# Gather and scatter of an expert name all 128 rows with a bound on the row number; no size variants, counts or branches in GpSimd's loop

## The chip, the cores and the metric

One Trainium2 chip, one of its cores. The metric is the device time of one launch, in microseconds. Three runs of the kernel before took 1130.07, 1128.4 and 1129.77 us; the median is 1129.77 us.

## The reference, cut to what matters

One layer of a streaming encoder over 512 tokens of width 1024. A mixing sub-layer (mLSTM heads and sparse attention heads behind one projection) comes first; the change does not touch it. The channel sub-layer is a mixture of 64 small experts, eight of which each token selects:

```
scores = sigmoid(hf @ w_router);  sel = scores + b_router
the 4 best of 8 groups of experts, then the 8 best experts in them -> eidx (512, 8)
gw = scores[eidx] / sum * 2.5
for each expert e, for its tokens tok:
    xb = hf[tok]
    u  = silu(xb @ w_gate[e]) * (xb @ w_up[e])        # 1024 -> 256
    y[tok] += (u @ w_down[e]) * gate                  # 256 -> 1024
out = x + gate2 * rms_norm(y + shared expert)
```

512 x 8 selections over 64 experts are 64 tokens for an expert on average. For the reference's inputs the smallest expert has 37 tokens and the largest 100. All is float32; the weights of one expert are 3 x 1024 x 256 x 4 B = 3.15 MB, which are read from HBM once.

## The kernel before, in words

Three stages run before the experts: `stage_in`, `stage_attention`, `stage_route`. The last computes the routing, stores the normalised tokens as rows in HBM (`G.h2_rows`, 512 rows of 4 KB), and leaves tables in SBUF: for each token and expert its place in that expert, and with `G.count_tab` (L1417, L2165) the number of tokens of each expert.

`stage_experts` (from L1534) runs the 64 experts in order; each engine has its own loop, eight experts to a turn (`UNROLL`, `turns` at L1678), and they meet through semaphores. An expert has a tile of 128 rows (`CAP`): its tokens stand in partitions 0 to n-1, the rest is padding. For an expert e:

- VectorE builds one-hot picks (L1881), TensorE finds the token and gate of each place with them (L2017), and `pick_rows` (L1578) writes the row numbers `sidx`: token number for a place that is taken, and 512 + partition for a place that is not.
- GpSimd gathers the rows from `h2_rows` into `xg` with an indirect DMA (`gather_rows`, L1586), four experts ahead. A row number over 511 is out of bounds, and the row is left as it is.
- TensorE transposes the rows (L2024), ScalarE and VectorE split them and the weights in a high and a low float32r part (L1802, L1810, L1901, L1905), TensorE multiplies by gate and up (L2034, 24 matmuls), transposes u (L2042) and multiplies by down (L2089, 8 matmuls). This always works on 128 rows, whatever the count.
- ScalarE and VectorE scale the two halves of the result into `yb` (L1851, L1954; two buffers, each waits for the scatter two experts before), and GpSimd scatters the rows with an accumulating indirect DMA into `G.y_sums` in HBM (`add_rows`, L1592). The scatter before has to have landed first (L1770), since two of them may add to one row.
- SyncE issues the weight loads: gate and up of expert e+4 in halves as the split of expert e is done (L1692 to L1697), down of e+3 after the down product of expert e-1 (L1702). Four slots hold weights.

The last two experts' results are not scattered but added on TensorE (L2134). Then y is read back and normalised.

In GpSimd's loop (L1759) each gather and each scatter is written eleven times, for 48, 56, 64, ... 120 and 128 rows (`SIZES`, L51). `count_of` loads the expert's count into a register (L1757), and `by_size` (L1745) picks the variant with a tree of three or four branches (L1751, L1753). A variant's row lists, source and destination are cut to that many partitions. A scatter has no bound on its row number: the padding within its size is added to rows 512 to 639 of `y_sums`, which nobody reads. The first four gathers (L1742), ahead of the loop, name all 128 rows.

Of the kernel before, what the change touches and what calls it, by code (L numbers as in the profile page):

```python
# [22 lines left out]
SEQ = 512  # L23
# [11 lines left out]
E_N = 64  # L35
# [10 lines left out]
CAP = P  # L46
MAX_EXTRA = SEQ * 8 // CAP
STEPS = (SEQ - 1) // CAP
MEAN = SEQ * 8 // E_N

SIZES = [*range(MEAN - 16, CAP, 8), CAP]  # L51

QK_W = 2 * HEADS * DH
# [1056 lines left out]
def stage_route(nc, A, G):  # L1111

    with ExitStack() as own:  # L1113
# [179 lines left out]
        def _(dve):  # L1293
# [120 lines left out]

            n_e, k_e, cum, at = (cnt[:, n, :] for n in range(4))
            step(nc.vector.tensor_copy(n_e, ps[:, 7, NT * E_N:(NT + 1) * E_N]))
            nc.vector.tensor_copy(G.count_tab[:, :], n_e[0:1, :])  # L1417
            step(nc.vector.tensor_scalar(k_e, n_e, float(CAP), None, ALU.is_gt))
            for m in range(2, STEPS + 1):
                step(nc.vector.scalar_tensor_tensor(k_e, n_e, float(m * CAP), k_e, ALU.is_gt, ALU.add))  # L1420
# [113 lines left out]
def stage_experts(nc, A, G):  # L1534

    with ExitStack() as own:
# [46 lines left out]
            q(nc.vector.tensor_scalar(pad[:, 0:1], f, 0.0, k[0:CAP, K_PADROW:K_PADROW + 1], ALU.is_equal, ALU.mult))  # L1583
            return nc.vector.scalar_tensor_tensor(sidx[:, n:n + 1], f, -1.0, pad[:, 0:1], ALU.add, ALU.add)

        def gather_rows(pool, slot, n, rows=CAP):  # L1586

            return pool.indirect_dma_start(out=xg[slot][0:rows, :], out_offset=None, in_=G.h2_rows,  # L1588
                                           in_offset=bass.IndirectOffsetOnAxis(ap=sidx[0:rows, n:n + 1], axis=0),
                                           bounds_check=SEQ - 1, oob_is_err=False)  # L1590

        def add_rows(pool, slot, n, rows=CAP):  # L1592

            return pool.indirect_dma_start(out=G.y_sums, out_offset=bass.IndirectOffsetOnAxis(ap=sidx[0:rows, n:n + 1], axis=0),  # L1594
                                           in_=yb[0:rows, slot, :], in_offset=None, compute_op=ALU.add)

# [1 line left out]
        with ExitStack() as inner:  # L1600
# [129 lines left out]
            @block.gpsimd  # L1730
            def _(pool):
                for n in range(RING - 1):
                    nc.gpsimd.memset(xg[n], 0.0).then_inc(s_zero, 1)
                for n in range(2):
                    pool.dma_start(G.y_sums[SEQ + n * 64:SEQ + (n + 1) * 64, :], G.xt[0:64, 0, :]).then_inc(s_sc, 16)
                for n in range(AHEAD):
                    if n == RING - 1:
                        pool.wait_ge(s_sdn, NT)
                        nc.gpsimd.memset(xg[n], 0.0).then_inc(s_zero, 1)
                    pool.wait_ge(s_zero, n + 1)  # L1740
                    pool.wait_ge(s_idx, n + 1)
                    gather_rows(pool, n, n).then_inc(s_g[n], 16)  # L1742
                pool.wait_ge(s_yw, 16 * NT)

                def by_size(count, sizes, move):  # L1745

                    if len(sizes) == 1:
                        move(sizes[0])
                        return
                    half = len(sizes) // 2  # L1750
                    with pool.If(count > sizes[half - 1]):  # L1751
                        by_size(count, sizes[half:], move)
                    with pool.Else():  # L1753
                        by_size(count, sizes[:half], move)

                def count_of(e):
                    return pool.value_load(G.count_tab[0:1, bass.ds(e, 1)], min_val=0, max_val=SEQ)  # L1757

                def step(t, n, ahead):  # L1759
                    e = UNROLL * t + n  # L1760
                    if ahead(AHEAD):
                        pool.wait_ge(s_idx, e + AHEAD + 1)
                        pool.wait_ge(s_xp, e + 1)
                        pool.sem_inc(s_passed, 1)
                        count = count_of(e + AHEAD)
                        by_size(count, SIZES, lambda rows: gather_rows(pool, n % RING, (n + AHEAD) % UNROLL, rows).then_inc(s_g[n % RING], 16))
                    if ahead(2):
                        pool.wait_ge(s_ya, e + 2)
                        pool.wait_ge(s_yd, e + 2)
                        pool.wait_ge(s_sc, SC0 + 16 * e)  # L1770
                        pool.sem_inc(s_passed, 1)
                        count = count_of(e)
                        by_size(count, SIZES, lambda rows: add_rows(pool, n % 2, n, rows).then_inc(s_sc, 16))

                turns(pool, step)
                pool.sem_inc(x_added, 1)

                def extra(j):
                    pool.wait_ge(x_idx, j + 1)
                    pool.sem_inc(s_passed, 1)  # L1780
                    gather_rows(pool, 1, 0).then_inc(x_g, 16)
                    pool.wait_ge(x_ya, j + 1)
                    pool.wait_ge(x_yd, j + 1)
                    pool.sem_inc(s_passed, 1)
                    pool.indirect_dma_start(out=G.y_sums, out_offset=bass.IndirectOffsetOnAxis(ap=sidx[:, 0:1], axis=0),
                                            in_=xyb, in_offset=None, compute_op=ALU.add).then_inc(x_sc, 16)
                    pool.wait_ge(x_sc, 16 * j + 16)
                    pool.sem_inc(x_added, 1)

                extra_tiles(pool, extra, adds=True)  # L1790
# [352 lines left out]
def build(nc, A, out):  # L2143
    with ExitStack() as ctx:
        def sb(name, shape, dt=F32):
            return ctx.enter_context(nc.sbuf_tensor(name, shape, dt))

        G = Shared()
        G.ps = ctx.enter_context(nc.psum_tensor("ps", [P, 8, 512], F32))
        G.k = sb("consts", [P, K_W])  # L2150
        G.gb = sb("gate_bias", [HEADS, 2])
        G.cs = sb("cs", [P, KC])
        G.cols = sb("cols", [P, 44])
        G.rows = sb("rows", [P, 4, D])
        G.maskb = sb("maskb", [P, NT, SEQ])
        G.xt = sb("xt", [P, NT, D])
        G.s_wgu = [ctx.enter_context(nc.semaphore(f"gate_up_landed{n}")) for n in range(RING)]
        G.s_wd = [ctx.enter_context(nc.semaphore(f"down_landed{n}")) for n in range(RING)]
        G.s_wout = ctx.enter_context(nc.semaphore("w_out_landed"))

        G.u_shared = G.rows[:, 0, :].rearrange("p (f t) -> p f t", f=FC)
        G.posm = sb("place_in_expert", [P, E_N * NT])
        G.gt = sb("token_and_gate", [P, E_N, NT, 6], BF16)
        G.extra_base = sb("extra_base", [P, P])
        G.count_tab = sb("expert_counts", [1, E_N], I32)  # L2165
        G.extra_tab = sb("extra_tab", [1, P + 1], I32)
        G.h2_rows = nc.dram_tensor("h2_rows", (SEQ, D), F32, kind="Internal").ap()
        G.y_sums = nc.dram_tensor("y_rows", (SEQ + P, D), F32, kind="Internal").ap()
        G.out = out

        G.QKC = NT * NAT_W
        G.main = sb("main", [P, G.QKC + 2 * HEADS * SEQ])
        G.side = sb("side", [P, 10240])
        G.nat = G.main[:, 0:G.QKC].rearrange("p (i n) -> p i n", i=NT)
        G.qkc = G.main[:, G.QKC:].rearrange("p (c t) -> p c t", c=2 * HEADS)
        G.w_shared_down = G.main[:, G.QKC + 2048:G.QKC + 4096].rearrange("p (f n) -> p f n", f=FC)
        G.wout = G.side[:, 0:8192].rearrange("p (f n) -> p f n", f=2 * HEADS)
        G.row_pieces = [G.side[:, 8192:10240].rearrange("p (c d) -> p c d", c=2), G.xt[:, 1:3, :]]
        G.top8, G.last_left = G.xt[:, 3, 64:72], G.xt[:, 3, 128:128 + SEQ]  # L2180
        G.gf, G.ga = G.rows[0:HEADS, 3, 0:SEQ], G.rows[0:HEADS, 3, SEQ:2 * SEQ]
        G.aN = G.posm[:, 0:2 * NT * HEADS].rearrange("p (a i h) -> p a i h", a=2, i=NT)
        G.w_gate_up = [t.rearrange("p (m c f) -> p m c f", m=2, c=KC)
                       for t in (G.side[:, 0:4096], G.side[:, 4096:8192], G.main[:, 0:4096], G.main[:, 4096:8192])]
        G.w_down = [t.rearrange("p (f n) -> p f n", f=FC) for t in (G.side[:, 8192:10240], G.main[:, G.QKC:G.QKC + 2048],
                                                                               G.maskb[:, :, :].rearrange("p i t -> p (i t)"),
                                                                               G.rows[:, 1:3, :].rearrange("p i d -> p (i d)"))]

        G.held = [ExitStack(), ExitStack()]
        stage_in(nc, A, G)  # L2190
        with ExitStack() as middle:
            G.arena = middle.enter_context(nc.sbuf_tensor("arena", [P, 6144], F32))
            G.catT = middle.enter_context(nc.sbuf_tensor("catT", [P, 2 * HEADS, SEQ], F32))
            stage_attention(nc, A, G)
            G.held[0].close()
            stage_route(nc, A, G)
            G.held[1].close()
        stage_experts(nc, A, G)
# [18 lines left out]
```

## Time and profile before

| what | us |
|---|---|
| median of three runs | 1129.77 |
| the profiled execution, its own time | 1132.51 |
| its span, first to last instruction | 1130.7 |
| TensorE busy | 1037.0 |
| VectorE busy | 836.9 |
| ScalarE busy | 521.8 |
| GpSimd busy | 234.5 |

The span is 1.8 us shorter than the execution's own time. The experts take the part of the span from about 415 to 1104 us. In the page's forty slices of 28.3 us the DMA engines' share is 9 tenths or more in nearly all of these, and TensorE's too. The share of the DMA engines is the mean over the core's 16; two transfers that one engine has open together both count, so it can read a little over 1.

### The profile page before, as it was taken

What the parts mean: (1) busy time and instruction counts of PE and PEld (TensorE: products, weight loads), DVE (VectorE), ACT (ScalarE), POOL (GpSimd) and SP (SyncE); (2) the same over time, 40 slices, a digit from 0 to 9 for tenths busy, and PEclk for the clock granted to TensorE, in tenths of its full rate; (3) what the DMA queues carried; (4) which work ended last, traced back from release to release, by engine and by line L of the source; (5) the groups of instructions that cost most, each with busy time, mean ns of one, the idle gap of its engine ahead of it and who ended that gap; (6) DMA issues with size and microseconds to landing.
All of it is one profiled execution on the core that took longest, in us unless ns stands there. A gap on an engine that the chain in (4) does not pass through costs nothing.

```text
span 1130.7 us, 16022 instructions
## 1 busy us (share of the span) xinstructions
PE 1037.0 (92%) x4777; PEld 733.0 (65%) x4778; DVE 836.9 (74%) x1480; ACT 521.8 (46%) x610; POOL 234.5 (21%) x145
## 2 busy tenths in 40 slices
PE   1899997978998989999998999999999999899995
PEld 1898887657446447766775666667766666566662
DVE  4887899886665457787876787778787776676865
ACT  3425463364111145555554554555555454545542
POOL 0000000100000034353321323423222222342210
PEclk9899998989996999999999999999999999999998
DMA  9775300600948078999999999999999999999944
GB/s 358 244 277 178 101 1 1 229 14 13 388 186 327 27 249 269 356 344 343 338 366 348 323 333 344 345 337 329 324 338 333 346 308 339 304 328 334 340 113 152
DMA packets 82999, 297.60 MB, mean 263 GB/s; under 512 B 10799, under 2 KB 23131, under 8 KB 73437
## 3 DMA queue, kind: packets, MB, share of 16 engines
q1 hardware_dynamic: 69188, 259.12, 63.6%
q0 software_dynamic: 12208, 34.62, 13.4%
q10 hardware_dynamic: 1514, 2.97, 0.7%
q14 instruction: 68, 0.56, 0.1%
q8 instruction: 21, 0.34, 0.1%
HBM read 274.71 MB, written 24.12 MB: 264 GB/s over the span
## 4 chain that ended last, share of the span: by engine, by line
DMA 37%; PE 13%; issue 7%; POOLq 3%; DVE 3%; SPq 2%; ACT 1%; POOL 0%; DVEq 0%; ACTq 0%
DMA y_rows<-yb,row_numbers 28%; PE ps L2034 6%; DMA side<-in_w_exp_up 5%; PE ps L2089 4%; DMA main<-in_w_exp_up 2%; POOLq L1757 2%; DMA xg<-h_rows,row_numbers 1%; SPq L1573 1%; PE ps L2024 1%; PE ps L2134 1%; POOLq L1751 1%; ACT w_gate_up_hi L1802 1%; DVE main L2008 0%; DVE w_gate_up_lo L1901 0%; DVE pick L1881 0%
## 5 line engine op out<-in xcount | busy, mean ns | idle before, releaser
L1901 DVE TENSOR_TENSOR w_gate_up_lo<-side,w_gate_up_hi 128x2048 fp32r<-128x2048 f32 x64 | 146.8, 2294 | 78.9 <-ACT w_gate_up_hi L1802 78.8
L1901 DVE TENSOR_TENSOR w_gate_up_lo<-main,w_gate_up_hi 128x2048 fp32r<-128x2048 f32 x64 | 146.7, 2292 | 71.9 <-ACT w_gate_up_hi L1802 71.8
L1594 POOL DMA_INDIRECT y_rows<-yb,row_numbers x62 | 116.2, 1874 | 375.3 <-issue 311.4
L1802 ACT ACTIVATE w_gate_up_hi<-side 128x2048 fp32r<-128x2048 f32 x64 | 122.1, 1910 | 95.5 <-DMA side<-in_w_exp_up 54.1
L1802 ACT ACTIVATE w_gate_up_hi<-main 128x2048 fp32r<-128x2048 f32 x64 | 122.2, 1910 | 91.5 <-PE ps L2034 45.8
L2034 PE MATMUL ps<-w_gate_up_hi,xT_hi 128*128 128x512 f32 x512 | 144.7, 404 | 11.8 <-DVE xT_lo L1905 8.7
L2034 PE MATMUL ps<-w_gate_up_hi,xT_lo 128*128 128x512 f32 x512 | 137.6, 390 | 0.0
L2034 PE MATMUL ps<-w_gate_up_lo,xT_hi 128*128 128x512 f32 x512 | 137.3, 390 | 0.0
L2034 PEld LDWEIGHTS ps<-w_gate_up_hi,xT_hi 128*128 128x128 f32 x512 | 91.4, 189 | 32.1 <-issue 14.2
L2034 PEld LDWEIGHTS ps<-w_gate_up_hi,xT_lo 128*128 128x128 f32 x512 | 96.2, 188 | 21.1
L2034 PEld LDWEIGHTS ps<-w_gate_up_lo,xT_hi 128*128 128x128 f32 x512 | 96.1, 188 | 21.0
L1588 POOL DMA_INDIRECT xg<-h_rows,row_numbers x48 | 81.4, 1695 | 86.6 <-issue 68.1
L1810 ACT ACTIVATE xT_hi<-ps 128x1024 fp32r<-128x1024 f32 x64 | 65.4, 1023 | 46.4 <-PE ps L2024 46.4
L1905 DVE TENSOR_TENSOR xT_lo<-ps,xT_hi 128x1024 fp32r<-128x1024 f32 x64 | 78.0, 1218 | 11.8 <-ACT xT_hi L1810 11.6
L1851 ACT ACTIVATE yb<-ps,found 128x512 f32<-128x512 f32 x64 | 43.9, 685 | 56.9 <-PE ps L2089 36.6
L2024 PE MATMUL ps<-consts,xg 128*128 128x128 f32 x384 | 55.6, 289 | 12.1 <-DMA xg<-h_rows,row_numbers 12.1
L1881 DVE TENSOR_SCALAR pick<-consts,place_in_expert 128x128 bf16<-128x128 f32 x256 | 63.1, 320 | 0.8 <-PEq L1113 0.8
L2089 PE MATMUL ps<-maskb,uT 128*128 128x512 f32 x128 | 60.7, 619 | 0.0
L2089 PE MATMUL ps<-rows,uT 128*128 128x512 f32 x128 | 57.7, 593 | 1.0 <-DVE uT L1914 1.0
L2089 PE MATMUL ps<-main,uT 128*128 128x512 f32 x128 | 57.6, 592 | 0.0
L2089 PE MATMUL ps<-side,uT 128*128 128x512 f32 x128 | 57.6, 593 | 0.0
L1451 PE MATMUL ps<-side,catT 128*128 128x512 f32 x128 | 55.5, 593 | 1.1 <-PEq L730 1.1
(309 smaller groups left out, 1554.9 us busy)
## 6 DMA issues: line engine op xcount, KB each, us to landing
side<-in_w_exp_gate SPq DMA_DIRECT2D x60, 512.0 KB, 9.6
side<-in_w_exp_up SPq DMA_DIRECT2D x60, 512.0 KB, 23.9
main<-in_w_exp_gate SPq DMA_DIRECT2D x60, 512.0 KB, 9.9
main<-in_w_exp_up SPq DMA_DIRECT2D x60, 512.0 KB, 24.6
side<-in_w_ada SPq DMA_DIRECT2D x20, 1024.0 KB, 7.7
main<-in_w_exp_down SPq DMA_DIRECT2D x16, 1024.0 KB, 23.1
maskb<-in_w_exp_down SPq DMA_DIRECT2D x16, 1024.0 KB, 20.4
side<-in_w_exp_down SPq DMA_DIRECT2D x16, 1024.0 KB, 23.6
```

Of the source, the lines that this page charges most:

```text
L1451: ins = nc.tensor.matmul(ps[:, 2 * i + half, :], catT[:, f, i * P:(i + 1) * P], wout[:, f, 512 * half:512 * (half + 1)], start=f == 0, sto ...
L1588: return pool.indirect_dma_start(out=xg[slot][0:rows, :], out_offset=None, in_=G.h2_rows, in_offset=bass.IndirectOffsetOnAxis(ap=sidx[0:ro ...
L1594: return pool.indirect_dma_start(out=G.y_sums, out_offset=bass.IndirectOffsetOnAxis(ap=sidx[0:rows, n:n + 1], axis=0), in_=yb[0:rows, slot ...
L1802: nc.scalar.activation(whi[:, half], wgu[n % RING][:, :, HALF * half:HALF * (half + 1), :] .rearrange("p m c f -> p c m f"), ACT.Copy).the ...
L1810: nc.scalar.activation(xhi[:, :, :], ps[:, 0:2, :].rearrange("p b (c t) -> p (b c) t", t=P)[:, :, 0:CAP], ACT.Copy).then_inc(s_xhi, 1)
L1851: nc.scalar.activation(yb[:, n % 2, 0:512], ps[0:CAP, 4, :], ACT.Copy, scale=found[:, n, 1:2]).then_inc(s_ya, 1)
L1881: ins = nc.vector.tensor_scalar(pick[:, slot, i, :], k[:, K_IOTA:K_IOTA + CAP], posm[:, bass.ds(NT * e + i, 1)], None, ALU.is_equal)
L1901: nc.vector.tensor_tensor(wlo[:, half], src, whi[:, half].bitcast(F32), ALU.subtract).then_inc(s_wlo, 1)
L1905: nc.vector.tensor_tensor(xlo[:, :, :], ps[:, 0:2, :].rearrange("p b (c t) -> p (b c) t", t=P)[:, :, 0:CAP], xhi[:, :, :].bitcast(F32), AL ...
L2024: ins = nc.tensor.transpose(ps[:, c // 4, (c % 4) * P:(c % 4) * P + CAP], xg[n % RING][:, c:D:KC], ident[0:CAP, 0:CAP])
L2034: ins = nc.tensor.matmul(ps[0:CAP, 2 + slot, :], xp[:, HALF * half + c, :], wp[:, half, c].rearrange("p m f -> p (m f)"), start=half == 0 ...
L2089: ins = nc.tensor.matmul(ps[0:CAP, 4 + half, :], uT[:, n % 2, f, :], wd[n % RING][:, f, 512 * half:512 * (half + 1)], start=f == 0, stop=f ...
```

## The change

The list of sizes, the table of counts, `count_of`, `by_size` and the branches go. Every gather and every scatter in the loop names all 128 rows, as the first four gathers did. The scatter gets the bound that the gather had: a row number over 511 is left out. Semaphores, waits, their order, and all the other engines' programs are the same, but for the one copy of the counts on VectorE.

```diff
-MEAN = SEQ * 8 // E_N
-
-SIZES = [*range(MEAN - 16, CAP, 8), CAP]
...
-            nc.vector.tensor_copy(G.count_tab[:, :], n_e[0:1, :])
...
-        def gather_rows(pool, slot, n, rows=CAP):
+        def gather_rows(pool, slot, n):
 
-            return pool.indirect_dma_start(out=xg[slot][0:rows, :], out_offset=None, in_=G.h2_rows,
-                                           in_offset=bass.IndirectOffsetOnAxis(ap=sidx[0:rows, n:n + 1], axis=0),
+            return pool.indirect_dma_start(out=xg[slot], out_offset=None, in_=G.h2_rows,
+                                           in_offset=bass.IndirectOffsetOnAxis(ap=sidx[:, n:n + 1], axis=0),
                                            bounds_check=SEQ - 1, oob_is_err=False)
 
-        def add_rows(pool, slot, n, rows=CAP):
+        def add_rows(pool, slot, n):
 
-            return pool.indirect_dma_start(out=G.y_sums, out_offset=bass.IndirectOffsetOnAxis(ap=sidx[0:rows, n:n + 1], axis=0),
-                                           in_=yb[0:rows, slot, :], in_offset=None, compute_op=ALU.add)
+            return pool.indirect_dma_start(out=G.y_sums, out_offset=bass.IndirectOffsetOnAxis(ap=sidx[:, n:n + 1], axis=0),
+                                           in_=yb[:, slot, :], in_offset=None, compute_op=ALU.add,
+                                           bounds_check=SEQ - 1, oob_is_err=False)
...
-                def by_size(count, sizes, move):
-
-                    if len(sizes) == 1:
-                        move(sizes[0])
-                        return
-                    half = len(sizes) // 2
-                    with pool.If(count > sizes[half - 1]):
-                        by_size(count, sizes[half:], move)
-                    with pool.Else():
-                        by_size(count, sizes[:half], move)
-
-                def count_of(e):
-                    return pool.value_load(G.count_tab[0:1, bass.ds(e, 1)], min_val=0, max_val=SEQ)
-
                 def step(t, n, ahead):
                     e = UNROLL * t + n
                     if ahead(AHEAD):
                         pool.wait_ge(s_idx, e + AHEAD + 1)
                         pool.wait_ge(s_xp, e + 1)
                         pool.sem_inc(s_passed, 1)
-                        count = count_of(e + AHEAD)
-                        by_size(count, SIZES, lambda rows: gather_rows(pool, n % RING, (n + AHEAD) % UNROLL, rows).then_inc(s_g[n % RING], 16))
+                        gather_rows(pool, n % RING, (n + AHEAD) % UNROLL).then_inc(s_g[n % RING], 16)
                     if ahead(2):
                         pool.wait_ge(s_ya, e + 2)
                         pool.wait_ge(s_yd, e + 2)
                         pool.wait_ge(s_sc, SC0 + 16 * e)
                         pool.sem_inc(s_passed, 1)
-                        count = count_of(e)
-                        by_size(count, SIZES, lambda rows: add_rows(pool, n % 2, n, rows).then_inc(s_sc, 16))
+                        add_rows(pool, n % 2, n).then_inc(s_sc, 16)
...
-        G.count_tab = sb("expert_counts", [1, E_N], I32)
```

## Rows read from the trace of the kernel before

**Rows 1.** The page: the span's slices, 28.3 us each, in tenths.
```profile
PE   1899997978998989999998999999999999899995
PEclk9899998989996999999999999999999999999998
DMA  9775300600948078999999999999999999999944
```

**Rows 2.** The page: the chain that ended last, by engine and by line.
```profile
DMA 37%; PE 13%; issue 7%; POOLq 3%; DVE 3%; SPq 2%; ACT 1%; POOL 0%; DVEq 0%; ACTq 0%
```

**Rows 3.** Timeline of TensorE, 433 to 470 and 1090 to 1092 us: start us, us, instruction.
```profile
433.43 1.18 PE L2034 MATMUL ps<-w_gate_up_hi,xT_hi 128*128 128x512 f32 x4
...
443.68 1.18 PE L2034 MATMUL ps<-w_gate_up_hi,xT_hi 128*128 128x512 f32 x4
...
464.14 1.18 PE L2034 MATMUL ps<-w_gate_up_hi,xT_hi 128*128 128x512 f32 x4
...
1090.83 1.18 PE L2034 MATMUL ps<-w_gate_up_hi,xT_hi 128*128 128x512 f32 x4
```

**Rows 4.** Stretches: us, busy of each engine (instructions), TensorE clock, DMA share, GB/s.
```profile
core 0: us, PE busy (x) PEld busy (x) DVE busy (x) ACT busy (x) POOL busy (x), PEclk, DMA share, GB/s
440.00:1060.00 620.00, 598.43 (x2635) 413.30 (x2633) 473.78 (x747) 330.51 (x287) 204.38 (x115) 0.99 1.02 336
600.00:700.00 100.00, 94.78 (x415) 65.90 (x414) 74.67 (x118) 52.65 (x46) 29.72 (x19) 0.97 1.01 342
```

**Rows 5.** Waits, 440 to 1100 us: waiter, releaser, us in total, times, longest.
```profile
ACT w_gate_up_hi L1802 <- DMA side<-in_w_exp_up: 54.1, 17, 6.6
ACT w_gate_up_hi L1802 <- DMA main<-in_w_exp_up: 45.7, 17, 5.3
PE ps L2024 <- DMA xg<-h_rows,row_numbers: 9.6, 4, 5.2
```

**Rows 6.** The chain from 460 to 500 us, one scatter to the next.
```profile
470.99 8.08 DMA y_rows<-yb,row_numbers
479.11 0.06 issue
479.17 0.30 POOLq L1757
479.48 0.03 issue
479.51 0.15 POOLq L1757
...
480.10 0.55 issue
...
480.90 7.95 DMA y_rows<-yb,row_numbers
```

**Rows 7.** The page: queue q0 is GpSimd's: packets, MB, share of 16 engines.
```profile
q1 hardware_dynamic: 69188, 259.12, 63.6%
q0 software_dynamic: 12208, 34.62, 13.4%
```

**Rows 8.** GpSimd's gather by its line, up to 420 us: four instructions that name 128 rows.
```profile
L1588 POOL DMA_INDIRECT xg<-h_rows,row_numbers x3: 1010/1134/2749, 401.5 to 405.0; - x3
L1588 POOL DMA_INDIRECT rows<-h_rows,row_numbers x1: 997/997/997, 416.0 to 416.0; - x1
DMA to landing us min/median/max: 4.0/8.1/10.4
```

**Rows 9.** The same line, 420 to 1110 us: sizes by count; ns min/median/max.
```profile
L1588 POOL DMA_INDIRECT xg<-h_rows,row_numbers x45: 956/1087/3117, 433.3 to 1060.8; - x45
DMA to landing us min/median/max: 6.9/9.3/13.0
```

**Rows 10.** The scatter's line, whole trace, then its last three (1080 to 1110 us).
```profile
L1594 POOL DMA_INDIRECT y_rows<-yb,row_numbers x62: 1389/1588/3484, 439.0 to 1098.7; - x62
...
DMA to landing us min/median/max: 4.2/8.6/11.6
...
L1594 POOL DMA_INDIRECT y_rows<-yb,row_numbers x3: 1396/1427/1435, 1083.5 to 1098.7; - x3
```

**Rows 11.** Stretches with one indirect transfer alone on the DMA engines, columns as in Rows 4.
```profile
417.80:418.90 1.10, 1.10 (x7) 0.91 (x5) 0.00 (x0) 1.10 (x1) 0.00 (x0) 1.00 0.46 123
1094.70:1096.50 1.80, 1.80 (x10) 1.48 (x9) 0.00 (x0) 0.00 (x0) 0.00 (x0) 1.00 0.73 100
1100.70:1103.00 2.30, 1.78 (x4) 0.87 (x5) 1.20 (x6) 0.02 (x1) 0.00 (x0) 1.00 0.96 135
```

**Rows 12.** Stretches with weight loads alone (1071), then loads beside indirect transfers (851).
```profile
1071.00:1074.00 3.00, 3.00 (x14) 2.44 (x14) 2.73 (x3) 0.63 (x2) 1.28 (x1) 1.00 1.04 418
851.50:853.00 1.50, 1.50 (x8) 0.78 (x7) 1.46 (x3) 1.12 (x2) 0.00 (x0) 1.00 1.09 298
```

## The prediction

> **What bounds the kernel now.** I read the slices first [rows 1]: from the fifteenth on, where the experts begin, both TensorE and the DMA engines stand at 9 tenths, so either could be the bound, and the chain that ended last says which to look at: DMA 37%, TensorE 13% [rows 2]. Then the pace of the experts. While the weight slots are still full, gate-and-up of one expert starts 10.25 us after that of the one before (433.43 to 443.68), and three starts take 30.71 us (433.43 to 464.14), 10.24 each [rows 3]. That is TensorE working without a pause. From the expert at 433.43 to the last one at 1090.83 there are 61 steps in 657.40 us, 10.78 each. So 0.54 us an expert, 33 us in all, is lost to something else. The stretch 440 to 1060 us has the DMA engines at a share of 1.02 and 336 GB/s [rows 4], and ScalarE, which touches the weights first, waits 100 us for the up weights in 34 waits [rows 5]. The weights arrive only as fast as they are used up. The experts are a balance: the DMA engines are full and set 10.78, with TensorE's 10.24 close under it.
>
> There is a third cycle of about that length. A scatter waits until the one before has landed: 470.99 issued, landed at 479.07, next issued at 480.90, 9.9 us from one to the next [rows 6]. It makes up most of the chain's DMA share. But its length is itself mostly queueing on full DMA engines: landing takes a median of 8.6 us in the loop and 4.2 at best [rows 10].
>
> **What an expert costs the DMA engines.** A stretch with weight loads alone moves 418 GB/s [rows 12], 26.1 GB/s for each of 16 engines. The weights of one expert, 3.146 MB or 196.6 KB an engine, then take 7.5 us. Queue q0 took 13.4% of 16 engines' span for 34.62 MB [rows 7]: 0.134 x 1130.7 = 151.5 us of each engine for 34.62 MB / 4096 B / 16 = 528 rows, so 0.287 us for a row, gather and accumulate together. 528 rows over 64 experts are 8.25 rows an engine and expert, 2.4 us. The sum is 9.9 us against 10.78 measured; the 0.9 us missing are engines that wait for one another and slow one another down. That they do is seen in a stretch of mixed traffic, 298 GB/s instead of 418 at a share of 1.09 [rows 12].
>
> **The change part by part.**
>
> *Which engines carry the rows.* This is the part that decides. The first four gathers already name 128 rows. The fourth was issued at 416.04 [rows 8], and for 1.1 us it is alone on the DMA engines: share 0.46, 123 GB/s, which is 135 KB or 33 rows [rows 11]. So about seven and a half of 16 engines work, though there are rows enough for all. Two scatters cut to their expert's size, likewise alone, have 0.73 and 0.96 over their whole length. 
>
> The Trainium skill ("DMA: Bandwidth & Descriptors", The descriptor swizzle) says the same of a plain transfer of 128 partitions: engine 0 serves partitions 0 to 3 and 32 to 35, engines 0 to 7 all of 0 to 63. It does not speak of indirect ones; the 0.46 agrees. By it engine 0 would have eight live rows in every expert with 36 tokens or more, and the smallest here has 37.
>
> The weights still go over all 16, and a load has landed only when the slowest engine has done its part. So the busiest engine sets the pace: 7.5 us of weights and 8 + 8 rows in place of 8.25. At 0.287 us a row that is 7.5 + 4.6 = 12.1 us an expert. Bounds: below, a row costs no more than its bytes, 4096 B at 26.1 GB/s = 0.157 us, so 7.5 + 2.5 = 10.0 us, under TensorE's 10.24, and nothing is lost (up to 0.54 us won). Above, the 0.9 us of mutual disturbance stay on top: 13.0 us. I take 12.2, just over the sum: the row price is already a loaded one, and the eight lighter engines leave more of HBM to the others, but the heavy ones never get a pause. That is 1.4 us an expert more. From 434 us on some 60 experts' loads are still to come, as four slots were filled before: 60 x 1.4 = 84 us.
>
> *Padding.* A scatter no longer writes its padding: 8452 rows in q0, less the live ones (2 x 4096, less 130 of the last two experts, which are not scattered) and less the 128 that clear the spare rows (L1735), leave 262, four an expert; at 0.287 / 16 us a row, 5 us in all if DMA bound. They fell on all engines, the busiest one no longer sees them, and the 16 rows above already leave them out. In exchange each transfer names some 60 places that are out of bounds. The fourth gather had over 80 of them and still landed within 4.0 us, the least of all gathers [rows 8], against 4.2 for the quickest scatter [rows 10]; no price is to be seen, and I take none. They also fall mostly on the idle half.
>
> *GpSimd's instructions.* A gather that names 128 rows takes 1.00 to 1.13 us, bar one of 2.75, and one cut to size 0.96 at least and 1.09 at the median [rows 8, 9]: nothing for naming more. The scatter with 128 rows isn't in the trace; between 1.43 us as now [rows 10] and twice that. It is 1.4 us at most on the scatter cycle.
>
> *Branches and counts.* From the landing at 479.07 to the next scatter at 480.90 go 1.83 us: two loads of the count, a tree of branches, 0.55 us of issue in one place [rows 6]. About 1.4 us of it go, for a scatter and likewise for a gather. With all cycles as before this would shorten the scatter's turn from 9.9 to 8.5 us. With the DMA engines as the bound at 12.2 it is covered, and what is late next is the weights, not the scatter. The same holds for TensorE's wait of 9.6 us in four gathers [rows 5], which come after the turn of GpSimd's long loop body: a shorter body may end them, and under 12.2 us an expert they would not show. The copy of the counts on VectorE is one small instruction in routing; zero.
>
> *The scatter's cycle after the change.* Its eight rows on engine 0 stand in one queue beside the weight packets. Landing was 8.6 us with four or five rows an engine, of which 2 to 3 us pass before the first packet; eight rows then land after some 10 to 12 us. It stays under or at the 12.2 us of the weights, without 1.4 us of branches. ScalarE's `yb` waits for the scatter two back and has over 20 us.
>
> **The rivals.**
>
> 1. *As forecast, 12.2 us an expert:* 1132.5 + 84 = 1216 us for the profiled execution; it lay 2.7 us over the median, so 1214. Within it 11.7 to 12.8 us an expert, 1184 to 1250.
> 2. *The same concentration, but a row costs little more than its bytes.* The lighter half of the engines frees HBM, and accumulates overlap with weight packets on one engine. Then 10.0 to 11.7 us: from 1125 up to 1184, 1155 in the middle. For it speaks the 418 GB/s of unmixed traffic, against it the 298 of mixed.
> 3. *Faster:* the sized transfers' spread is kept, since the rows of an indirect scatter may be dealt to engines in another way than a gather's. Then nothing is concentrated, or only half of it; the scatter's turn is 1.4 us shorter, gathers start earlier, and the padding's 5 us are saved. The place is L1594's issue, the price at most the 0.54 us over TensorE's floor, 33 us. It decides if the DMA share stays at 1.0 in the experts; half the saving gives 1113 us. Against it: the 0.46.
> 4. *Heavier:* disturbance stays, the scatter's cycle with twice the rows becomes the longest at 13 us or more, and TensorE, waiting in every expert, loses clock: it was 0.97 where it waited most [rows 4]. 13.3 us an expert: 1132.5 + 150 = 1280.
> 5. *The edit does nothing on the DMA side*, as sized transfers were already dealt out by fixed partitions. Then only the saved branches stay, under a DMA bound: 1125. The sized scatters' 0.73 and 0.96 speak against it; I count it with the third.
>
> **How the numbers follow.** The forecast has 0.55, the second 0.2, the faster ones (3 and 5) 0.13, the heavier 0.12. The predicted time is the forecast's, 1212 with a little off for gathers that are no longer late. The range leaves out the faster case and the far end of the heavier: 1142 to 1268. A measurement of this kernel tells 0.2%, 2.3 us, from no change. Of the second case 0.03 lies within that and 0.01 under it. So faster 0.14, same 0.03, slower 0.83.
>
> **What would show it.** Right: the DMA share in the experts falls from 1.02 to 0.75 to 0.85 though the kernel waits for weights more; GB/s from 336 to about 290; ScalarE's waits for the up weights grow from 100 us to 150 or more; gates-and-up start 12.2 us apart; landing of scatter and gather grows to 10 us and more; TensorE's waits rise by 80 us. The GpSimd instructions stay at 1.0 and 1.5 us, and from landing to next scatter it is about 0.5 us. Wrong: a share still at 1.0, or a pace at or under 10.8. If the pace is 12 us but the share also stays at 1.0, the out-of-bounds places cost time, and not the dealing out. If landings are long and the weights are on time, the scatter's cycle is the bound.

## The result, and the profile after

The changed kernel takes 1164.59 us (median of four, 1162.01 to 1165.81) against 1129.92 us before: 1.030 times as long, 95% interval 1.0281 to 1.0327. It is slower, as forecast, but by 35 us and not by 82. It lies inside the range of 1142 to 1268, but in the second case of the rivals (1125 to 1184), not in the first.

The slices of the page of the kernel after, 29 us each, answer to [rows 1]:

```profile
PE   1899998979989989999999999989898999999985
DMA  9775200603955269999999999999999989999934
```

Busy time by stretches, for 440 to 1060 us (us, busy of each engine with its instructions, TensorE clock, DMA share, GB/s), answers to [rows 4]. The DMA share fell from 1.02 to 0.93 and the traffic from 336 to 319 GB/s, and TensorE is busy for 582 us instead of 598:

```profile
440.00:1060.00 620.00, 582.02 (x2549) 397.55 (x2548) 454.47 (x716) 313.88 (x277) 190.87 (x110) 1.00 0.93 319
```

TensorE's timeline, first matmul group of gate-and-up, answers to [rows 3]. The start of one expert at 434.89 and the next at 445.13 are the 10.24 us of full weight slots; from 434.89 to the last expert at 1120.61 there are 61 steps in 685.72 us, 11.24 each, where it was 10.78. 61 x 0.46 = 28 us of the span's 31:

```profile
434.89 1.18 PE L2015 MATMUL ps<-w_gate_up_hi,xT_hi 128*128 128x512 f32 x4
...
445.13 1.18 PE L2015 MATMUL ps<-w_gate_up_hi,xT_hi 128*128 128x512 f32 x4
...
1120.61 1.15 PE L2015 MATMUL ps<-w_gate_up_hi,xT_hi 128*128 128x512 f32 x4 [0.67 <-issue]
```

The waits from 440 to 1130 us (waiter, releaser, us in total, times, longest) answer to [rows 5]. Weights are waited for 153 us instead of 100, and a second wait has grown beside them, ScalarE's for a free `yb`, 121 us (from 440 to 1060 us it is 116 us, and was 19):

```profile
ACT yb L1832 <- DMA y_rows<-yb,row_numbers: 121.2, 48, 5.4
ACT w_gate_up_hi L1783 <- DMA main<-in_w_exp_up: 79.6, 33, 4.5
ACT w_gate_up_hi L1783 <- DMA side<-in_w_exp_up: 73.2, 29, 4.7
PE ps L2005 <- DMA xg<-h_rows,row_numbers: 7.6, 11, 1.5
```

The chain from 520 to 560 us answers to [rows 6]. From the landing at 536.88 to the next scatter at 537.75 it is 0.87 us, in place of 1.83, and the branches are gone from between; but the scatter itself lands after 10.3 to 11.4 us:

```profile
526.38 10.50 DMA y_rows<-yb,row_numbers
536.88 0.03 issue
...
537.01 0.51 issue
...
537.75 11.40 DMA y_rows<-yb,row_numbers
549.15 0.02 issue
```

That holds for this stretch. Over the whole span the scatters are a smaller part of the chain than they were, and the weight loads, with SyncE's issue of them (L1569), a larger one. From 700 to 760 us that issue is 50.8% of the chain, the scatters 16.5%. The page's line of before, then that of after:

```profile
DMA y_rows<-yb,row_numbers 28%; PE ps L2034 6%; DMA side<-in_w_exp_up 5%; PE ps L2089 4%; DMA main<-in_w_exp_up 2%; POOLq L1757 2%; DMA xg<-h_rows,row_numbers 1%; SPq L1573 1%; PE ps L2024 1%; PE ps L2134 1%; POOLq L1751 1%; ACT w_gate_up_hi L1802 1%; DVE main L2008 0%; DVE w_gate_up_lo L1901 0%; DVE pick L1881 0%
```

```profile
DMA y_rows<-yb,row_numbers 17%; SPq L1569 12%; DMA main<-in_w_exp_up 9%; PE ps L2015 6%; DMA side<-in_w_exp_up 4%; PE ps L2070 3%; SPq L1572 2%; DMA xg<-h_rows,row_numbers 2%; PE ps L2005 1%; ACT w_gate_up_hi L1783 1%; DVE w_gate_up_lo L1882 1%; DVE xT_lo L1886 1%; PE ps L2115 0%; DVE main L1989 0%; PE ps L2033 0%
```

The page's queues and the gather's and scatter's own lines (ns min/median/max; then us from issue to landing, the gather's from 420 us on) answer to [rows 7, 9, 10]. Queue q0 moves 1.02 MB less, about 250 rows of padding (by the experts' token counts it is 258). It has 6096 packets more, though it moves less; e10 below shows that a place out of bounds is a small packet. The instructions take what they took. Landings grow from 8.6 to 10.4 us for the scatter and from 9.3 to 11.1 for the gather:

```profile
q1 hardware_dynamic: 69188, 259.12, 61.2%
q0 software_dynamic: 18304, 33.60, 11.5%
...
L1584 POOL DMA_INDIRECT xg<-h_rows,row_numbers x45: 996/1038/3078, 433.3 to 1090.4; - x45
...
DMA to landing us min/median/max: 4.2/11.1/11.7
...
L1590 POOL DMA_INDIRECT y_rows<-yb,row_numbers x62: 1549/1609/3437, 439.2 to 1130.4; - x62
...
DMA to landing us min/median/max: 6.2/10.4/12.5
```

### The profile page after: what moved, and what is told of

It is laid out like the page before. It is cut to its first block, busy times and chain, and to the rows that moved or that the text cites. A ratio compares the mean times of both kernels' runs of the same rounds, so it can differ in the third digit from the quotient of the medians.

```text
span 1161.9 us, 15132 instructions
## 1 busy us (share of the span) xinstructions
PE 1047.5 (90%) x4777; PEld 733.4 (63%) x4778; DVE 834.7 (72%) x1479; ACT 517.1 (45%) x610; POOL 231.2 (20%) x144
## 2 busy tenths in 40 slices
DMA packets 89045, 296.18 MB, mean 255 GB/s; under 512 B 17153, under 2 KB 29485, under 8 KB 79533
## 3 DMA queue, kind: packets, MB, share of 16 engines
q0 software_dynamic: 18304, 33.60, 11.5%
HBM read 289.32 MB, written 39.32 MB: 283 GB/s over the span
## 4 chain that ended last, share of the span: by engine, by line
DMA 32%; SPq 14%; PE 11%; issue 4%; DVE 3%; ACT 1%; POOLq 0%; DVEq 0%; POOL 0%; ACTq 0%
DMA y_rows<-yb,row_numbers 17%; SPq L1569 12%; DMA main<-in_w_exp_up 9%; PE ps L2015 6%; DMA side<-in_w_exp_up 4%; PE ps L2070 3%; SPq L1572 2%; DMA xg<-h_rows,row_numbers 2%; PE ps L2005 1%; ACT w_gate_up_hi L1783 1%; DVE w_gate_up_lo L1882 1%; DVE xT_lo L1886 1%; PE ps L2115 0%; DVE main L1989 0%; PE ps L2033 0%
## 5 line engine op out<-in xcount | busy, mean ns | idle before, releaser
L1584 POOL DMA_INDIRECT xg<-h_rows,row_numbers x48 | 76.9, 1603 | 37.3 <-DVE row_numbers L1580 24.2
L1935 DVE TENSOR_SCALAR yb<-ps,found 128x512 f32<-128x512 f32 x64 | 47.7, 745 | 25.1 <-DMA y_rows<-yb,row_numbers 23.3
L2070 PE MATMUL ps<-maskb,uT 128*128 128x512 f32 x128 | 57.6, 592 | 0.0
```

What stands on the lines that cost most here:

```text
L1584: return pool.indirect_dma_start(out=xg[slot], out_offset=None, in_=G.h2_rows, in_offset=bass.IndirectOffsetOnAxis(ap=sidx[:, n:n + 1], ax ...
L1935: nc.vector.tensor_scalar(yb[:, n % 2, 512:D], ps[0:CAP, 5, :], found[:, n, 1:2], None, ALU.mult).then_inc(s_yd, 1)
L2070: ins = nc.tensor.matmul(ps[0:CAP, 4 + half, :], uT[:, n % 2, f, :], wd[n % RING][:, f, 512 * half:512 * (half + 1)], start=f == 0, stop=f ...
```

## The experiments

Three theories stood after the result. A: in a transfer of 128 rows the live ones stand on half of the engines, and the busiest engine's load sets the pace. B: the scatter's own turn, that is its landing and the issue of the next one, is the bound. C: the places out of bounds cost the time. Every run is compared with the kernel before, run on the same chip; "pace" is the mean distance of the 61 steps of gate-and-up, read from TensorE's timeline as above. It is that of the one profiled execution, which for e3 was a quick one, 1110.5 us.

| run | rows of the busiest engine, an expert | branches | us | ratio to before, 95% interval | pace, us |
|---|---|---|---|---|---|
| before | cut to size | yes | 1129.9 | | 10.78 |
| after | 8.0 + 8.0 | no | 1164.6 | 1.0304 [1.0281, 1.0327] | 11.24 |
| e1_spread | 4.5 + 4.5 | no | 1099.8 | 0.9743 [0.9722, 0.9764] | 10.24 |
| e2_branches_128 | 8.0 + 8.0 | yes | 1207.4 | 1.0696 [1.0674, 1.0718] | 11.98 |
| e3_gather_128 | 8.0 + cut to size | scatter's | 1119.4 | 0.9907 [0.9855, 0.9960] | 10.36 |
| e4_scatter_128 | cut to size + 8.0 | gather's | 1178.8 | 1.0440 [1.0408, 1.0473] | 11.49 |
| e5_by_eights | 7.6 + 7.6 | no | 1154.7 | 1.0229 [1.0192, 1.0266] | 11.10 |
| e6_two_sums | 8.0 + 8.0 | no | 1168.8 | 1.0349 [1.0315, 1.0383] | 11.30 |
| e7_two_sums_spread | 4.5 + 4.5 | no | 1101.2 | 0.9749 [0.9717, 0.9781] | 10.24 |
| e8_spread_branches | 4.5 + 4.5 | yes | 1134.8 | 1.0054 [1.0009, 1.0099] | 10.82 |
| e9_two_sums_half_down | 8.0 + 8.0, less weights | no | 1101.3 | 0.9746 [0.9708, 0.9784] | 10.24 |
| e10_live_padding | 8.0 + 8.0 | no | 1160.2 | 1.0271 [1.0237, 1.0305] | 11.19 |
| e11_live_padding_spread | 8.0 + 4.5 | no | 1101.3 | 0.9746 [0.9713, 0.9780] | 10.24 |
| e12_ten_engines | 6.7 + 6.7 | no | 1122.3 | 0.9933 [0.9906, 0.9960] | 10.63 |

The rows of the busiest engine, gathered and scattered, are counted from the experts' token counts and the dealing that the Trainium skill states ("DMA: Bandwidth & Descriptors", The descriptor swizzle): engine 8*(p>>6) + ((p>>2)&7) for partition p. It states this for a plain transfer; that it holds for the indirect ones here is what e1, e5 and e12 test. How transfers that are cut to size are dealt, no run tests; some 4 rows an engine is their even share.

**e1_spread.** Only the order in which an expert's tokens are dealt to partitions changes. The list lies in the constants and is loaded over a mask that the experts no longer need.

```diff
+    k[:, K_W:] = (16 * ((i & 3) + 4 * ((i >> 5) & 1)) + 8 * (i >> 6) + ((i >> 2) & 7))[None, :]
...
+            sp.dma_start(G.k[:, K_TRI:K_TRI + P], A["consts"][:, K_W:K_W + P]).then_inc(s_in, 16)
...
-                        ins = nc.vector.tensor_scalar(pick[:, slot, i, :], k[:, K_IOTA:K_IOTA + CAP],
+                        ins = nc.vector.tensor_scalar(pick[:, slot, i, :], k[:, K_TRI:K_TRI + CAP],
```

> The kernel after, but places are dealt to partitions so that live rows stand on all engines: partition p holds place 16*((p&3)+4*((p>>5)&1)) + 8*(p>>6) + ((p>>2)&7), the picks compare against this list instead of 0 to 127. Still 128 rows named, same padding, same bound, same waits. Theory A (in a transfer of 128 rows the live ones fall on half the engines, and the busiest sets the pace): back to the time of before or under it, 1100 to 1130 us, DMA share in the experts back at about 1.0, landing of a scatter at 7 to 9 us. Theory C (the out-of-bounds places cost the time): stays at 1160 to 1168 us. Theory B (not the engines' load but the scatter's own turn, landing plus issue, is the bound): depends on the landing; if it falls from 10.3 to 8.6 us, TensorE's pace and 1100 us.

Measured: 1099.75 us, under both kernels. The stretch 440 to 1060 us of this kernel has TensorE busy for all of its 620 us:

```profile
440.00:1060.00 620.00, 620.00 (x2775) 433.68 (x2775) 499.59 (x774) 352.16 (x303) 163.10 (x119) 1.00 0.98 346
```

and in its waits the weights are no longer among what ScalarE waits for:

```profile
ACT w_gate_up_hi L1785 <- PE ps L2017: 134.4, 60, 2.4
...
POOL y_rows L1592 <- DMA y_rows<-yb,row_numbers: 81.8, 16, 6.2
...
ACT yb L1834 <- PE ps L2072: 42.0, 61, 0.7
```

Names, padding and bounds are those of the kernel after, so C falls. Where the live rows stand costs 65 us of the 1164.6. A and B both allow 1100 us; e6 and e9 part them.

**e2_branches_128.** The tree of the kernel before, with 128 in every leaf. The gather's call is changed likewise, and the scatter has the bound:

```diff
-                        by_size(count, SIZES, lambda rows: add_rows(pool, n % 2, n, rows).then_inc(s_sc, 16))
+                        by_size(count, SIZES, lambda rows: add_rows(pool, n % 2, n, CAP).then_inc(s_sc, 16))
```

> The kernel before with its counts and branches, but every branch names 128 rows, and the scatter has the bound: the change without the removal of branches. It puts about 1.3 us back between a landing and the next scatter. Theory A (engines' load sets the pace of 11.3 us): 1162 to 1175 us, the branches are covered. Theory B (the scatter's turn, 10.3 us landing + 0.9 us, is the bound): 60 x 1.3 = 78 us more, 1225 to 1245 us.

Measured: 1207.43 us, 43 more than after: between the two. The branches are not covered. The chain from 700 to 760 us shows the turn, 10.23 us of landing and from 744.52 to 746.50 another 1.98 us; from 440 to 1060 us ScalarE waits 216 us for `yb` and not at all for weights. Here the turn is the bound.

```profile
734.29 10.23 DMA y_rows<-yb,row_numbers
744.56 0.07 issue
744.69 0.30 POOLq L1758
745.02 0.15 POOLq L1758
...
745.75 0.52 issue
...
746.50 10.59 DMA y_rows<-yb,row_numbers
```

```profile
ACT yb L1852 <- DMA y_rows<-yb,row_numbers: 216.3, 48, 7.1
ACT w_gate_up_hi L1803 <- PE ps L2035: 17.9, 10, 2.2
```

**e3_gather_128 and e4_scatter_128.** Each half of the change alone: one of the two calls is that of the kernel after (in e4 with its bound), the other keeps its tree.

```diff
# e3
-                        count = count_of(e + AHEAD)
-                        by_size(count, SIZES, lambda rows: gather_rows(pool, n % RING, (n + AHEAD) % UNROLL, rows).then_inc(s_g[n % RING], 16))
+                        gather_rows(pool, n % RING, (n + AHEAD) % UNROLL).then_inc(s_g[n % RING], 16)
# e4
-                        count = count_of(e)
-                        by_size(count, SIZES, lambda rows: add_rows(pool, n % 2, n, rows).then_inc(s_sc, 16))
+                        add_rows(pool, n % 2, n).then_inc(s_sc, 16)
```

> The kernel before, but the gather alone names 128 rows and has no branches; the scatter stays cut to size with its branches. Theory A: the busiest engine carries 8 + 4 rows, 7.5 + 12 x 0.235 = 10.3 us by the price that 11.26 us of the kernel after gives, so with the 0.9 of disturbance at most 11.0: 1125 to 1148 us. Theory C: half the loss, 1147 us. Theory B: the scatter's landing hardly changes, 1130 us.

> The kernel before, but the scatter alone names 128 rows, with the bound and without branches; the gather stays cut to size with its branches. Theory A: 1130 to 1150 us, a little over the gather's case since an accumulated row costs more than a plain one. Theory B: nearly all of the loss, 1155 to 1165 us. Theory C: half, 1147 us.

Measured: the gather's half alone is a little faster than before, 1119.39 us, though its runs scatter from 1108.6 to 1124.1. That is under every range given; none of them counted the gather's branches, which are gone in it, and what they are worth was not tried alone. The scatter's half alone is slower than the whole change, 1178.78 us, beyond all three. The asymmetry fits B in kind, since only the scatter has a turn; it would fit as well if an added row cost more than a gathered one, and no run prices the two apart. But e4 has some 4 rows less on the busiest engine than the kernel after and no branch in the scatter's turn, and is 14 us slower. What its delayed gathers do to it was not followed further: TensorE waits 17 us for them in five waits. That stays open.

**e5_by_eights.** The list `16 * (i % 8) + i // 8` in place of the first.

> As the spread kernel, but another list: partition p holds place 16*(p%8) + p//8. If an engine of a 128-row transfer has eight neighbouring partitions, this spreads the live rows as evenly as could be: 1100 us like the spread kernel. If it has two groups of four, partitions 4k..4k+3 and 32 further on (theory A in the form that the Trainium skill gives it), 64 live rows stand in the lower half of each eight, all of them on every second engine, 8 on each: as slow as the kernel after, 1160 to 1168 us.

Measured: 1154.66 us, 10 under the kernel after and 55 over the spread one. The same edit with another list is slow, so it is the dealing and not the edit. Engines with eight neighbouring partitions would have made it fast. It is a little under the range, for a reason that the expectation overlooked: an expert of under 64 tokens has fewer than 8 rows on each of the eight engines, 486 on the busiest over all 64 experts (7.6 each) against 512 (8.0).

**e6_two_sums and e7_two_sums_spread.** Two arrays of sums, so that a scatter waits for the one two before it, by the semaphore of its parity. The final sum reads one array alone: the odd experts' part is left out of the output.

```diff
-            return pool.indirect_dma_start(out=G.y_sums, ...
+            return pool.indirect_dma_start(out=(G.y_sums, G.y_sums2)[slot], ...
...
-                        pool.wait_ge(s_sc, SC0 + 16 * e)
+                        wait_scattered(pool, n, UNROLL // 2 * t + n // 2)
```

> The kernel after with two arrays of sums in HBM, one for the even experts and one for the odd: a scatter then waits for the scatter two before it, not for the one just before. The shared expert's rows are stored to both (2 MB more, ahead of the loop), and the final sum reads the even array alone, so the odd experts' part is missing from the output. Rows are still on half of the engines. Theory A (the busiest engine's load is the bound): 1160 to 1170 us. Theory B (the scatter's turn is the bound): the turn's wait is gone and the pace falls to TensorE's 10.24 or to what the weights allow, at most 11.0 us: 1105 to 1145 us.

> The spread kernel with the same two arrays of sums: it tells what the two arrays cost by themselves. TensorE is busy without a pause in the spread kernel, so nothing is left to win: 1098 to 1108 us by both theories.

Measured: 1168.8 and 1101.15 us. The two arrays by themselves cost next to nothing (e7 against e1, both at a pace of 10.24). Against the kernel after the first gains nothing. ScalarE's waits in it (440 to 1060 us) have lost the one for the scatter, and the weights have taken it over, 215 us:

```profile
ACT w_gate_up_hi L1790 <- DMA side<-in_w_exp_up: 107.6, 23, 6.5
ACT w_gate_up_hi L1790 <- DMA main<-in_w_exp_up: 107.0, 22, 6.7
...
ACT yb L1840 <- PE ps L2080: 19.0, 33, 0.7
```

So in the kernel after the turn is not what holds the pace, though the chain runs along it in places: without it the weights give the same pace (11.30). The turn is as long, 10.4 + 0.87 us, so taking it away gains nothing. B holds for e2 and not here.

**e8_spread_branches.** e2 with the list of e1.

> The spread kernel with counts and branches put back, every branch naming 128 rows: against the spread kernel it gives the price of the branches when rows are on all engines, against the kernel before the price of the sized transfers. Theory B: a turn of some 7.5 to 8.5 us landing + 2 us, about TensorE's 10.24: 1100 to 1115 us. Theory A: the branches are covered, 1100 us.

Measured: 1134.81 us (1127.18 to 1141.84), over both ranges. The landings on its chain from 700 to 760 us take 8.6 to 9.7 us, not 8, and with some 2 us from landing to issue a turn is 10.5 us at least; the pace is 10.82. Branches thus cost 35 us where rows are spread and 43 where they are not. Naming 128 rows, spread, instead of sizes costs 0.5% by this (1.0054 [1.0009, 1.0099]).

**e9_two_sums_half_down.** To e6 comes this edit, which leaves half of an expert's down weights out.

```diff
-            eng.dma_start(wd[slot], w_down[e].rearrange("(p f) n -> p f n", f=FC)).then_inc(s_wd, 16)
+            eng.dma_start(wd[slot][:, 0:1, :], w_down[e].rearrange("(p f) n -> p f n", f=FC)[:, 0:1, :]).then_inc(s_wd, 16)
```

> The kernel of the two sums (no turn to wait for, rows on half the engines, 1169 us), and the loop's down loads bring only half of an expert's down weights, 0.52 MB less an expert; the product is made with what lies in the other half, and the final sum still leaves the odd experts out. If the busiest engine's load is the bound (theory A), it falls by 33 KB or 1.26 us an expert, from 11.29 to 10.0, under TensorE's 10.24: 1100 to 1110 us. If the bound is something else in the chain of gather, scatter and products (their latencies), 1155 to 1170 us.

Measured: 1101.31 us. Gathers, scatters and products take the same form, and TensorE has no pause left from 440 to 1060 us. The load of the engines was the bound.

**e10_live_padding and e11_live_padding_spread.** The padding of every gather is read from 128 further rows of the token array, which are filled ahead of the loop in place of the sums' spare rows.

```diff
-                                           bounds_check=SEQ - 1, oob_is_err=False)
+                                           bounds_check=SEQ + P - 1, oob_is_err=False)
```

> The kernel after, but the gather's padding is live: the 128 row numbers from 512 on name 128 more rows of the token array (bound 639), so every gather moves 128 rows, eight on each of 16 engines. The scatter is as it was. The busiest engines carry 8 + 8 rows as before, the others 8 + 0 more: 0.26 MB more an expert in all. Theory A (only the busiest engine counts): 1160 to 1175 us. If the total that the DMA engines or HBM move is the bound: 7% more, some 0.8 us an expert, 1205 to 1220 us.

> The spread kernel with the same live padding: every engine carries 8 gathered and about 4.4 scattered rows. Theory A, with 0.235 us a row: 7.5 + 12.4 x 0.235 = 10.4 us an expert, just over TensorE's 10.24: 1100 to 1120 us. Against the kernel with live padding and no spread, which moves the same bytes, it is faster by 45 to 70 us; if the total is the bound, they are alike.

Measured: 1160.16 and 1101.27 us. q0 moves 50.36 MB instead of 33.60 in both; the stretch 440 to 1060 us of the one and of the other:

```profile
440.00:1060.00 620.00, 583.46 (x2547) 397.80 (x2546) 457.12 (x722) 316.30 (x277) 198.75 (x109) 1.00 0.98 344
```

```profile
440.00:1060.00 620.00, 620.00 (x2780) 433.77 (x2780) 498.55 (x773) 352.87 (x304) 164.84 (x120) 1.00 1.00 372
```

16.8 MB more on engines that have room cost nothing (a ratio to before of 1.0271, where the kernel after has 1.0304), and the same bytes, evenly dealt, run at 372 GB/s. It isn't the total, and not HBM: it is the busiest engine.

The pages of the kernel after and of e10 also show what a place out of bounds is. The 4096 that become live rows take 4095 packets under 512 B with them, and the number of packets stays: one small packet a place. Against the kernel before that does not come out whole: 7538 places more are out of bounds in the kernel after, and it has 6354 small packets more (17153 against 10799). What the other small packets of the transfers cut to size are stays open. The line of after, then that of e10:

```profile
DMA packets 89045, 296.18 MB, mean 255 GB/s; under 512 B 17153, under 2 KB 29485, under 8 KB 79533
```

```profile
DMA packets 89046, 312.94 MB, mean 271 GB/s; under 512 B 13058, under 2 KB 25390, under 8 KB 79534
```

**e12_ten_engines.** A list that deals the first 80 places to ten engines.

> As the spread kernel, but its list deals the first 80 places to ten engines in turn and the rest to the other six. The busiest engine then has 427 rows of the 64 experts in each direction, 6.7 an expert, against 8.0 in the kernel after (11.24 us an expert) and 7.6 in the one dealt by eights (11.10). Theory A says a pace between theirs and TensorE's floor, and it prices the row: by the difference of those two, 0.17 us, 11.24 - 2 x 1.33 x 0.17 = 10.79 us and 1137 us; by (11.24 - 7.5) / 16 = 0.234 us, 10.62 us and 1127 us; by the forecast's 0.287 us, 10.48 us and 1118 us. If not the busiest engine but the number of engines with rows counted in steps, or only the half-and-half split, it would be 1100 or 1160 us.

Measured: 1122.31 us (1118.73 to 1126.84), pace 10.63. The pace falls by 0.61 us for 2.66 rows less, 0.23 us a row. With e5 between them the points do not lie on one line (0.17 from 8.0 to 7.6, 0.26 from there to 6.7). But the runs of e12 itself lie 8 us apart, 0.13 us of pace, so that the 0.23 is good to some 0.03.

## Why the prediction was right or wrong

*What bounds the kernel before:* "the DMA engines are full and set 10.78" is not borne out. At 0.23 us a row their load is 7.5 + 8.25 x 0.23 = 9.4 us, under TensorE's 10.24. The chain of before runs along the scatter's turn [rows 6], and e8, which has its branches and nearly its rows an engine, has its pace (10.82), while e1, which differs from e8 by the branches alone, has 10.24. So the 0.54 us over the floor were most likely the turn with its branches. Against it stand ScalarE's waits for the up weights in before [rows 5], which e8 has not. No run takes the branches out of the kernel that is cut to size, so this is argued.

*Which engines carry the rows:* right. A share of 0.46 in a stretch of 1.1 us [rows 11] was enough to see it, and it decides the sign. e1, e5, e10, e11 and e12 confirm it.

*What an expert costs the DMA engines:* this failed, at "7.5 + 4.6 = 12.1 us" and "I take 12.2". It is 11.24, and 11.30 without the turn. The row was mis-sized: 0.287 us came from the queue's busy share [rows 7], while e12, which moves rows off the busiest engine, gives 0.23. 7.5 + 16 x 0.23 = 11.2. The same page row in the kernel after gives 0.115 x 1161.9 us / 513 rows = 0.26. That rows are cheaper because half the engines have room is what the second rival said, and e11 speaks against it as the reason: there all 16 engines carry 8 + 4.5 rows, and 0.287 us a row would give 11.1 us, but the pace is 10.24, so a row costs at most (10.24 - 7.5) / 12.5 = 0.22 us (with fewer added than gathered rows). Why the busy share puts a row too high stays open. The last 0.1 us was my rounding up for "no pause". 0.96 us too much for 60 experts are 58 us. Against it stand 3 us at the two ends of the experts' stretch, which the sum did not have, and some 8 us of rounding and of profiled executions against medians, which leaves the error of 47.

*Branches:* this failed as well. They were put at nothing: "With the DMA engines as the bound at 12.2 it is covered". That cover was the mis-sized term's. The runs: without the removal of the branches the same transfers take 1207 us, by the turn of 12.0 (e2). So the removal gives 43 us back, and it would have stood in the sum, had the sum had 11.24 in it. Taken in the order of the runs e8, e1, after, the change is +6 us for naming 128 rows, -35 for the branches, +65 for where the live rows stand. The scatter's cycle was forecast to stay "under or at" the weights' pace with landings of 10 to 12 us: they are 10.4, and with branches it would have been over.

*Padding and GpSimd's instructions:* right. About 250 rows gone (262 forecast), out-of-bounds places without a price that shows (e1 has as many as the kernel after, and TensorE has no pause from 440 to 1060 us), 1.04 and 1.61 us for the instructions. From landing to issue 0.87 us remain, where about 0.5 was forecast.

*The signs to look for:* waits for up weights 153 us (150 or more), landings 10.4 and 11.1 (10 and more): as said. The share at 0.93 and 319 GB/s are between "right" and "wrong": the experts come faster than forecast, so the other half of the engines is not as idle. TensorE's pauses from 440 to 1060 us rose by 16 us (busy 582 in place of 598), where 80 over all experts were forecast.

*The rivals:* the second came out, and I gave it 0.2. Its range was the better one; its reason is not borne out, as said above. The third, faster, had the right price for the floor (33 us for TensorE's 10.24), and it is what another order of the rows makes of the change. The fourth, heavier, had TensorE's granted clock fall with its pauses, "0.97 where it waited most". In the kernel before, of the stretches of 100 us, it waited most from 900 to 1000 us (busy 91.80 us), at 1.00; in the kernel after the clock is 1.00 from 440 to 1060 us with 38 us of pauses, and in e2 0.97 with 67.

## What to carry to other kernels

Ask of every DMA that names a full tile with padding which engines carry its live rows: the load of the busiest one counts, not the bytes. If the rows may stand in any order, deal them so that any prefix is spread; here that turns a loss of 3% into a gain of 2.6% (1099.75 us, 0.9743 [0.9722, 0.9764]) with the simpler code. And where two cycles are nearly as long, price a removal under each of them: what is "covered" by a bound that was estimated is only as sure as the estimate.

## What the runs showed of the hardware that was not expected

The page's line on HBM traffic goes by what the instructions name, not by what moves. By it more was written after than before, 39.32 MB instead of 24.12, while queue q0 moved 1.02 MB less. e10 has the figures of after again, though its q0 moved 16.76 MB more. The line of before, then that of after:

```profile
HBM read 274.71 MB, written 24.12 MB: 264 GB/s over the span
```

```profile
HBM read 289.32 MB, written 39.32 MB: 283 GB/s over the span
```

A DMA share of 1.00 as the mean of 16 engines with 372 GB/s (e11) lets TensorE work without a pause, and 0.93 with 319 GB/s (after) does not. The mean share says nothing of the busiest engine.
